# Two products of a chunked scan change places in TensorE's queue: y from the state ahead of the state's own product

## The reference

```python
def wkv_scan(state, r, w, k, v, a, b, reverse):
    def step(s, inp):
        r_t, w_t, k_t, v_t, a_t, b_t = inp
        sa = jnp.einsum('bhij,bhj->bhi', s, a_t)
        s = s * w_t[:, :, None, :] + sa[..., None] * b_t[:, :, None, :] + v_t[..., None] * k_t[:, :, None, :]
        return s, jnp.einsum('bhij,bhj->bhi', s, r_t)
    tm = lambda t: jnp.swapaxes(t, 0, 1).astype(jnp.float32)
    state, y = lax.scan(step, state, tuple(tm(t) for t in (r, w, k, v, a, b)), reverse=reverse)
    return state, jnp.swapaxes(y, 0, 1)
...
    for n, rev in enumerate((False, True)):
        s_ctx, yc = run_scan(state0, fc, n, rev)
        _, yl = run_scan(s_ctx, fl, n, rev)
```

## Time and profile before

| what | value |
|---|---|
| median of 3 runs | 2237.53 us (2236.88 to 2239.69) |
| span of the profiled execution | 2236.4 us |
| the scan in it | from about 1193 to 2091 us |
| latent periods | 64 |
| TensorE busy | 2129.4 us (95%) |
| VectorE busy | 1177.5 us (53%) |
| ScalarE busy | 774.6 us (35%) |
| GpSimd busy | 647.4 us (29%) |

### The profile page before, as it was taken

How to read it: one execution, slowest core, us unless ns; L and a number is a source line. 1 busy time by engine, 2 the same in 40 slices (tenths; PEclk the granted TensorE clock), 3 DMA queues, 4 the chain that set the end, 5 groups by cost and what they waited for, 6 DMA issues and landing times. The chain is left out here.

```text
span 2236.4 us, 56049 instructions
## 1 busy us (share of the span) xinstructions
PE 2129.4 (95%) x23756; PEld 1368.9 (61%) x23756; DVE 1177.5 (53%) x2284; ACT 774.6 (35%) x2065; POOL 647.4 (29%) x901
## 2 busy tenths in 40 slices
PE   7999999999999999999896999999999999999798
PEld 3556565354444455444345888888888888888443
DVE  5443343134946770042624666666666666666674
ACT  4111111143255522210113444444444444444332
POOL 1010010023033410011123545444545444444011
PEclk9999999999999999999997999999999999999899
DMA  9201003701037766555314334533333333333742
GB/s 353 79 19 38 19 19 122 273 29 38 31 95 191 208 167 188 163 169 195 127 57 123 91 95 119 139 92 94 93 93 92 97 90 101 86 102 73 231 118 110
DMA packets 315866, 258.17 MB, mean 115 GB/s; under 512 B 138849, under 2 KB 272225, under 8 KB 312162
## 3 DMA queue, kind: packets, MB, share of 16 engines
q1 hardware_dynamic: 315618, 254.59, 37.9%
HBM read 174.80 MB, written 79.69 MB: 114 GB/s over the span
## 5 line engine op out<-in xcount | busy, mean ns | idle before, releaser
L1019 PE MATMUL ps<-xt,w_slab 128*128 128x512 f32 (+1 forms) x800 | 297.5, 526 | 0.0
L2168 PE MATMUL ps<-M,AT 64*64 64x64 f32 x6400 | 264.2, 224 | 7.6 <-ACT M L1957 4.4
L1883 POOL TENSOR_TENSOR SP<-Q,decay 64x128 f32<-64x128 f32 x304 | 128.7, 423 | 428.1 <-DVE Q L2086 399.6
L2168 PEld LDWEIGHTS ps<-M,AT 64*64 64x64 f32 x6400 | 219.3, 135 | 46.5 <-issue 14.6
L1019 PEld LDWEIGHTS ps<-xt,w_slab 128*128 128x128 f32 x800 | 148.3, 190 | 146.3 <-issue 122.6
L2168 PE MATMUL ps<-TT,MT 64*64 64x64 f32 x5120 | 215.6, 223 | 8.5 <-DVE TT L2029 1.3
L2168 PEld LDWEIGHTS ps<-TT,MT 64*64 64x64 f32 x5120 | 178.0, 135 | 39.6 <-issue 30.3
L2029 DVE COPY_PREDICATED TT<-mask,ps 128x128 f32<-128x128 int32 x400 | 125.1, 319 | 91.0 <-PE ps L2168 85.3
L2075 DVE STREAM_TRANSPOSE MT<-M 128x256 f32<-128x256 f32 x240 | 106.1, 442 | 125.8 <-ACT M L1957 123.8
L2161 PE MATMUL ps<-ar,bk 64*128 64x192 f32 (+1 forms) x1280 | 142.4, 342 | 14.3 <-POOL ar L1901 14.3
L645 PE MATMUL ps<-h,fgo 128*128 128x512 f32 x320 | 141.6, 597 | 2.4 <-PEq L202 2.4
(11 more groups left out here) (291 smaller groups left out, 3592.3 us busy)
## 6 DMA issues: line engine op xcount, KB each, us to landing
feat<-feature_scratch SPq DMA_DIRECT2D x160, 256.0 KB, 3.2
feature_scratch<-k_feats SPq DMA_DIRECT2D x64, 320.0 KB, 5.2
feature_scratch<-k_feats SPq DMA_DIRECT2D x24, 640.0 KB, 6.8
k_feats<-in_modw SPq DMA_DIRECT2D x8, 1536.0 KB, 6.7
w_slab<-in_rwin SPq DMA_DIRECT2D x24, 512.0 KB, 6.9
Q<-v_token_scratch SPq DMA_DIRECT2D x320, 32.0 KB, 2.5
Z<-v_token_scratch SPq DMA_DIRECT2D x320, 32.0 KB, 2.4
fgo<-in_modw SPq DMA_DIRECT2D x8, 1024.0 KB, 8.2
```

The lines of the kernel that those rows point to most:

```text
L1019: mm = pe.matmul(ps[:, bank, 0:n], (w1t if i is None else w[:, i % 2])[:, k, :], src[:, k, a:a + n], start=k == 0, stop=k == KT - 1)
L1883: g.tensor_tensor(SP[own(h)], turn(sub, Q[l][own(h), h]), pend_turn(c, own(h), sub).unsqueeze(2).broadcast_to([HD, NDIR, CK]), ALU.mult).t ...
L2168: mm = pe.matmul(out[o, b, :], L[o, b, :], R[o, b, :], start=True, stop=True)
```

## The change

In the first half-step of a latent period the call of `y_state` stands ahead of that of `state`. For context chunks, where there is no y, nothing changes.

```diff
                     products(j, a, 1)
                 if B_:
                     m(j, b, 8)
+                if lat:
+                    y_state(j, c, 0)
                 if Q_:
                     state(j, c, 0)
                 if lat:
-                    y_state(j, c, 0)
                     y(j, c, 0)
                     r(j, c, 1)
                 if B_:
```

## The result

The changed kernel takes 2254.23 us (median of 4 runs, 2250.40 to 2256.55), the kernel before 2238.34 on the same chip. The ratio on record is 1.0076, with a 95% interval of 1.0061 to 1.0091: 0.76% slower, some 17 us (the two medians as they stand differ by 15.9). The forecast was 2252.4 us, 15 us and 0.67%.

The account below looks back on a forecast made before the run. TensorE's order of work, with the few answers it waits for, was taken to set the period. 63 x 0.23 us plus 0.38 for the last period gave 14.9 us, so 2252.4 us, 0.67% slower; range 2248 to 2262.

Parts of the forecast that it names:

- The wait for Z: First half-step: y from the state now waits first for ScalarE's copy of sa; cost zero, covered by m8 with 0.6 us in hand.
- m8 to y from the state 0.47, to the state product 0.38, instead of 0.62: TensorE, first half-step: the state product's load starts 0.85 us behind m8 instead of 0.62, so 0.23 us later.
- From the state product to r 1.23: First half-step: the time from the state product's weight load to r's load stays 1.23 us.
- Nothing later absorbs it: Rest of the latent period: everything behind the state product moves with it, so the 0.23 us delay comes through.
- Periods and waits: Latent period goes from 11.24 to 11.47 us; r's wait for Q grows from 10.2 to some 43 us in all.
- The last period 0.38: Last latent period, with no m8 ahead: the move costs the full 0.38 us.
- The sum: 63 periods at 0.23 us give 14.5 us; with the last period, 14.9 us together.
- Q, r, the transposes and t2 do: Behind the state product: VectorE's adds start 0.23 us later, and so do Q, r, the transposes and t2.
- The pause that stays: Rival: y from the state cannot move up to m8; 0.38 us in all 64 periods, 24.3 us, 2261.9; chance 0.10, part or full.
- the absorbed delay: Rival: a later TensorE wait, for VectorE's mask before mt32, shrinks by 0.23 us; time stays 2237.5 us; chance 0.05.
- The faster case: Rival: two pauses of 0.15 us fewer make 63 periods 0.30 us shorter, 18.9 us, 2218.6; chance 0.03.

## Why the prediction was right, point by point

- *The wait for Z costs nothing.* Right: y from the state starts 0.46 behind m8, with no wait named before it.
- *m8 to y from the state 0.47, to the state product 0.38, instead of 0.62.* Right, 0.46 and 0.39. The pause of 0.15 comes with the change of rows between the groups, as the second half-step had shown. Rows are not all of it: sa is followed by the products of line 2161 in 0.38 us too (1503.51 to 1503.89), and there both have 64 rows, but the stationary matrices go from 64 to 128 columns. The row of that group in the kernel before:

```profile
1503.89 0.63 PEld L2161 LDWEIGHTS ps<-ar,bk 64*128 64x128 f32 x8
```

  The simple count, one group moved ahead is one group later (0.38), would have given 24.3 us, outside the measured 13.6 to 20.4 (the interval of the ratio times 2237.5).
- *From the state product to r 1.23.* Right: 1.23 in the change, with both parts of y ahead (1.24), and with the value part first (1507.64 - 1506.41 = 1.23).
- *Nothing later absorbs it.* Right. The wait of the last group for VectorE's mask stayed at 0.25 to 0.26, and a delay of 0.46 a period came through in full.
- *Periods and waits.* 11.47 forecast, 11.48 measured; r's wait 43 us in all forecast, 43.9 measured.
- *The last period 0.38.* Right: the state product there starts at 2100.57, y from the state at 2100.19 where Z came.
- *The sum.* 14.9 us forecast, 16.3 us measured in the scan, 17 by the ratio of the runs. The step that was short is the one on VectorE: "Q, r, the transposes and t2 do" move by 0.23 holds in 56 periods (and in the last of all, with its 0.38). In the last chunk of seven pairs it was 0.63, because the masked copy between those transposes came to stand behind a GpSimd operation. Seven times 0.40 is 2.8 us, which the sum had no term for: I had read one middle period and took the last chunk for the same. With it the sum is 17.7. Of that the profiled executions show 16.3, as the one before was held up in five half-steps where the one after was not (0.08 to 0.63 us more than their like, some 1.3 us together). The same 1.3 us are missing against the execution before when the change is left out of the last chunk (11.6 instead of 12.9). The largest is a stop of TensorE in the middle of a group:

```profile
1400.60 0.48 PEld L2168 LDWEIGHTS ps<-TT,MT 64*64 64x64 f32 x13 [0.20 <-issue]
1401.61 0.19 PEld L2168 LDWEIGHTS ps<-TT,MT 64*64 64x64 f32 x3 [0.53 <-issue]
```

  TensorE waited for nothing there that the profile shows; what makes this stop is open, and no run varies it. The next largest, 0.45 us, has a cause that shows. VectorE waited 2.76 us for a load of features, and what hangs on it through ScalarE reached TensorE late (0.77 us of waiting, 0.33 at the same place after the change, where the load was in time):

```profile
1446.72 0.42 DVE L2035 TENSOR_TENSOR_SCAN cum<-scan_tab,feat 128x128 f32<-128x128 f32 x1 [2.76 <-DMA feat<-feature_scratch]
...
1449.83 0.25 PEld L2168 LDWEIGHTS ps<-M,AT 64*64 64x64 f32 x6 [0.77 <-ACT M L1957]
```

- *Rivals.* The pause that stays and the absorbed delay are both excluded. The faster case needed the way to r to fall below 1.00 us; it never moved. The opposite order, the state product ahead of m8, shows where the gain was to be had: not between the state product and r, but ahead of it.

## What to carry to other kernels

In a queue with a fixed order, what stands ahead of the producer of a chain that another engine idles for is paid in full, and what stands between it and its consumer is free until the wait there is used up. So before an independent group is moved, find the producer that another engine idles for, and move groups behind it, not ahead of it. And look at the odd iteration too, the first or the last of a loop: there another engine works at another time, and a shift of 0.2 us can put two operations onto each other.

## What the runs showed of the hardware

- TensorE, float32, groups of small products at a granted clock of 1.00: a group of 8 passes takes 0.23 us until the next one with the same shape of stationary matrix, and 0.15 more where its number of rows changes between 128 and 64, either way (0.38), or its columns from 64 to 128 (0.38 from sa to line 2161). Semaphores that have been met add nothing that shows: sa, with three on its first instruction, follows t8 in 0.46, as y from the state, with one, follows m16 in 0.47.
- A masked copy of VectorE with both inputs in SBUF (0.41 us alone) and a multiplication on GpSimd (0.68 alone) wait for each other: 0.90 and 0.68 when GpSimd was first by 0.09, 0.49 and 0.87 when VectorE was first by 0.15. The copy ended 0.30 to 0.31 behind the end of the GpSimd operation in which it started, in all 56 last chunks of the eight executions without a hold. Holding GpSimd back by a semaphore brought the copy to at most 0.45.
- An operation of VectorE that need not wait can start before the shown end of the one ahead of it: the adds by 0.08 us behind line 2053 (1511.54 against 1510.74 + 0.88), but the transpose behind the adds 0.03 after their end (1506.57 against 1505.93 + 0.61). An idle time read from a timeline understated here by 0.08 what an earlier input brought.
